# Encoder block on one core: turns and the norm's spread ahead of the first column sums, the first scale summed as columns, another order of loads, two ring slots filled early

## The chip, the cores and the metric

The kernel runs on one core of a Trainium2 chip. The metric is the device time of one execution in microseconds; for one core that is the time of this core. Its engines are TensorE (PE), VectorE (DVE), ScalarE (ACT), GpSimd (POOL) and SyncE (SP). SP and POOL issue the loads. Every engine works through its own instructions in order and waits on semaphores for the others.

## What is computed

One layer of a streaming-encoder block on x of 512 tokens by 1024, conditioned on a vector c:

```python
mod = (silu(c) @ ada_w + ada_b).reshape(b, 9, 1024)   # sh1, sc1, g1, sh2, sc2, g2, sh3, sc3, g3
h = rmsnorm(x, norm_ffn1_g) * (1 + sc1) + sh1
x = x + 0.5 * g1 * ((silu(h @ w1) * (h @ w3)) @ w2)   # 1024 -> 2816 -> 1024
h = rmsnorm(x, norm_mix_g) * (1 + sc2) + sh2
...                                                   # projection, short conv, 4-head attention, projection
h = rmsnorm(x, norm_ffn2_g) * (1 + sc3) + sh3
x = x + 0.5 * g3 * ((silu(h @ v1) * (h @ v3)) @ v2)
return rmsnorm(x, final_norm_g)
```

All is float32. The change touches the beginning alone: `silu(c) @ ada_w` for sc1 and sh1, the first norm, and the first tiles of `h @ w1` and `h @ w3`.

## The kernel before

The model dimension lies on the partitions, in eight tiles of 128 by 512 tokens. A product of full precision is made of three products on operands split into a high part (rounded, made by ACT) and a low part (the rest, made by DVE): `three`, L860. A unit is a weight tile of 128 by 1024 (`raw`, loaded by SP at L320; `wh`, its high part, L437 or L548; `wl`, its low part, L1400). Unit n alternates between two buffers, so the load of unit n waits for the low part of unit n-2. The up part of the first FFN takes two units per output tile: tile 0 is units 0 and 1, tile 1 is units 2 and 3, and so on.

The opening makes the modulation of the first FFN. `ada_start` holds sc1 and sh1's weights in four groups g: 0 and 1 are the halves of the scale sc1, 2 and 3 the halves of the shift sh1. Each group comes in four loads of 512 KB (L310), each with two of the eight k tiles. Of groups 0 and 1 the even k are PE's and the odd k are DVE's; of groups 2 and 3 all k are DVE's.

- DVE's share is `start_chunk` (L1623 for the first k, L1626 for the others): it adds `ada_start * silu_c` into `acc`. Each chunk waits for the one before it of its group.
- PE's share is `start_rows` (L1006): a product with one column of `silu_c` as the stationary operand and 512 moving columns, which gives one row of 512. ACT copies the row to `ada_rows` (`row_copy`, L543), and PE turns it into four columns with four products of one partition (L1018).
- `start_sum` (L1018 and L1023) adds the sums over `acc` as columns, and `start_mod` (L1634, L1642) on DVE makes `mods` and the norm's factors `a_cols` of it.

Tile 0 is computed from the norm without the shift (`plain_u`, L1651, makes it; `plain_steps`, L1032, are its float32 products on `raw_first`), and the shift's share is added later by `bias_step` (L1049). Tile 1 is `second_steps`: three products per k on `hh` (ACT, `shifted_hi`, L552) and `hl` (DVE, `shifted_lo`, L1657), which need the shift. Tiles 2 to 21 follow in a loop (`up_tile`).

PE also turns x (`turn_x`, L983): six of the eight tiles as the tokens land, the last two (`turn_last`) when ACT has copied the banks they need. It turns the small vectors (bias, gains) that POOL loads into `vec1` and `vec2` (L1059, L1061), and spreads the norm's factors over the partitions (`norm_spread`, L901).

POOL loads the other modulation weights into a ring of four slots (`ada_ring`, L402), 512 KB each, which DVE works through in the loop (L1466, L1468). The first four of these loads wait for `bias_done`, the last bias step, since the tile `raw_first` lies on slots 0 and 1 of the ring:

```python
(raw_first,), _ = place(region + 2 * FT * 4 * SEQ, ("raw_first", [P, 2, UW], F32))   # the ring's address
...
pool.wait_ge(bias_done, 1)
with pool.Fori(0, N_MOD - 2) as j:
    for k in range(DT):
```

The order of all this is written out by hand, engine by engine; there is no planner.

Of the kernel before, what the change touches and what calls it, by code (L numbers as in the profile page):

```python
# [26 lines left out]
P = 128  # L27
# [9 lines left out]
UW = 1024  # L37
# [60 lines left out]
def hybrid_block(nc, x, c, positions, ada_w, ada_b, norm_ffn1_g, ffn1_w1, ffn1_w3, ffn1_w2, norm_mix_g,  # L98
                 w_in, conv_w, q_norm_g, w_uq, kv_norm_g, w_ukv, out_norm_g, w_out, norm_ffn2_g,
                 ffn2_w1, ffn2_w3, ffn2_w2, final_norm_g, consts, out):  # L100
    with ExitStack() as ctx:
# [74 lines left out]
        (raw_first,), _ = place(region + 2 * FT * 4 * SEQ, ("raw_first", [P, 2, UW], F32))  # L176
# [122 lines left out]
        def _(sp):  # L299
# [5 lines left out]
            def start_load(g):  # L305
# [3 lines left out]
                for i in range(4):  # L309
                    sp.dma_start(ada_start[:, DT * v + 2 * i:DT * v + 2 * i + 2, half * HALF_COLS:(half + 1) * HALF_COLS],  # L310
                                 adav[:, 2 * i:2 * i + 2, col:col + HALF_COLS]).then_inc(start_landed[g][i], 16)
# [25 lines left out]
            start_load(1)  # L337
            sp.dma_start(raw_first[:, 1, :].rearrange("p (k f) -> p k f", k=DT), w3v[0][:, :, 0:P]).then_inc(first_landed[1], 16)
            start_load(2)
            start_load(3)  # L340
            load(U_A1 + 2, 0, w1v[0][:, :, P:2 * P])
            load(U_A1 + 3, 1, w3v[0][:, :, P:2 * P])
# [39 lines left out]
        def _(pool):  # L382
# [14 lines left out]
            pool.wait_ge(bias_done, 1)  # L397
            with pool.Fori(0, N_MOD - 2) as j:
                for k in range(DT):

                    pool.wait_ge(ada_step, ADA_START + j * DT + k - 3)
# [29 lines left out]
        def _(act):  # L431
# [106 lines left out]
            def row_copy(g):  # L538

                act.wait_ge(row_done, g + 1)  # L540
                if g > 0:
                    act.wait_ge(ada_direct, g)
                act.activation(ada_rows[0:1, :], pb[ROW_BANK[g]][0:1, :], ACT.Copy).then_inc(row_copied, 1)  # L543

# [9 lines left out]
            for k in range(DT - 2):  # L554
                copy_x(k)
            row_copy(0)
            copy_x(DT - 2)
            copy_x(DT - 1)
            row_copy(1)
# [294 lines left out]
        def _(pe):  # L854
# [146 lines left out]
            def start_rows(g, ks):  # L1001

                v, half = divmod(g, 2)
                for k in ks:
                    pe.wait_ge(start_landed[g][k // 2], 16)
                    ins = pe.matmul(pb[ROW_BANK[g]][0:1, :], silu_c[:, k:k + 1],  # L1006
                                    ada_start[:, DT * v + k, half * HALF_COLS:(half + 1) * HALF_COLS],
                                    start=k == ADA_ON_PE[g][0], stop=k == ADA_ON_PE[g][-1])
                    if k == ADA_ON_PE[g][-1]:
                        ins.then_inc(row_done, 1)  # L1010

            def start_sum(g):

                half = g % 2
                if g < 2:
                    pe.wait_ge(row_copied, g + 1)
                    for col in range(HALF):
                        pe.matmul(pb[ROW_BANK[g]][:, col:col + 1], ada_rows[0:1, col * P:(col + 1) * P], one_col[0:1, :],  # L1018
                                  start=col == 0, stop=False, skip_group_check=True)
# [26 lines left out]
            def bias_step(k):  # L1046

                for b in range(2):
# [3 lines left out]

            pe.wait_ge(siluc_ready, 1)
            start_rows(0, ADA_ON_PE[0])
            turn_last(DT - 2)
            turn_last(DT - 1)
# [5 lines left out]
                         ident[0:V_COLS - V_ROWS1, 0:V_COLS - V_ROWS1]).then_inc(vec_turned, 1)  # L1062
            pe.wait_ge(consts_landed, 16)
            start_sum(0)
            pe.wait_ge(vec_ready, 3)
            norm_spread(N_FFN1)
            pe.wait_ge(x_copied, 3)
            start_rows(1, ADA_ON_PE[1])
            pe.wait_ge(x_copied, 6)
            plain_steps(0, (0,))  # L1070
            start_sum(1)
            plain_steps(0, (1, 2, 3))
# [324 lines left out]
        def _(dve):  # L1397
# [263 lines left out]
            for k in ADA_ON_DVE[0]:  # L1661
                start_chunk(0, k)
# [3 lines left out]
            dve.wait_ge(vec_ready, 3)  # L1666
            start_chunk(1, 1)
            start_mod(0)
            start_chunk(1, 3)
            plain_u(0)  # L1670
            start_chunk(1, 5)
            plain_u(1)
            start_chunk(1, 7)
            plain_u(2)
            plain_u(3)
# [5 lines left out]
            for k in range(2, DT):  # L1681
# [406 lines left out]
```

## Time and profile before

| | |
|---|---|
| median of 3 runs | 1006.18 us (1004.42 to 1006.41) |
| the profiled execution | 1003.93 us |
| its span, first to last instruction | 1002.3 us |
| PE busy | 983.8 us |
| DVE busy | 549.4 us |
| ACT busy | 349.9 us |
| POOL busy | 51.9 us |
| bytes moved by DMA | 128.93 MB |

The span is that of the profiled execution; the rows below are all from it, in microseconds from its start. In a timeline a row is a run of like instructions of an engine: when it starts, how long it takes from the start of the first to the end of the last, the engine (SPq is SP's queue), the source line, the operation, the tiles, how many instructions, and in brackets how long the engine was idle before it and what ended that. A float32 product is recorded as two matmuls. Matmuls overlap at their ends, so the time of a step is best read from start to start.

### The profile page before, as it was taken

What the parts mean: (1) busy time and instruction counts of PE and PEld (TensorE: products, weight loads), DVE (VectorE), ACT (ScalarE), POOL (GpSimd) and SP (SyncE); (2) the same over time, 40 slices, a digit from 0 to 9 for tenths busy, and PEclk for the clock granted to TensorE, in tenths of its full rate; (3) what the DMA queues carried; (4) which work ended last, traced back from release to release, by engine and by line L of the source; (5) the groups of instructions that cost most, each with busy time, mean ns of one, the idle gap of its engine ahead of it and who ended that gap; (6) DMA issues with size and microseconds to landing.
All of it is one profiled execution on the core that took longest, in us unless ns stands there. A gap on an engine that the chain in (4) does not pass through costs nothing.

```text
span 1002.3 us, 13157 instructions
## 1 busy us (share of the span) xinstructions
PE 983.8 (98%) x4524; PEld 807.8 (81%) x4524; DVE 549.4 (55%) x772; ACT 349.9 (35%) x542; POOL 51.9 (5%) x79
## 2 busy tenths in 40 slices
PE   7999999999999999999999999999999999999997
PEld 4678888888888888888888887788888888888886
DVE  3867876787676445754475548754334344433332
ACT  5243323232342232531256534533323223323222
POOL 2011111011000000000000320000000000000000
PEclk9999999999999999999999999999999999999999
DMA  9757866686453333233221212232333323333232
GB/s 328 247 183 237 272 200 207 202 270 214 140 177 98 97 97 99 75 84 101 68 70 41 85 43 85 84 105 85 103 97 91 105 85 103 96 96 96 81 113 85
DMA packets 180493, 128.93 MB, mean 129 GB/s; under 512 B 5376, under 2 KB 168002, under 8 KB 180464
## 3 DMA queue, kind: packets, MB, share of 16 engines
q1 hardware_dynamic: 172064, 98.98, 33.1%
q0 software_dynamic: 8400, 29.58, 8.9%
q8 instruction: 17, 0.28, 0.1%
q14 instruction: 12, 0.10, 0.0%
HBM read 126.44 MB, written 2.10 MB: 128 GB/s over the span
## 4 chain that ended last, share of the span: by engine, by line
PE 89%; DVE 4%; SPq 2%; DMA 2%; ACT 1%; issue 1%; DVEq 0%; ACTq 0%
PE pb L860 86%; DMA raw<-in_ffn_w_dram 2%; SPq L310 2%; DVE wl L1400 1%; PE pb L901 1%; DVE hl L1432 1%; DVE ubuf L1439 1%; ACT wh L437 1%; PE pb L883 0%; PE pb L1380 0%; DVE ptl L1921 0%; PE pb L1191 0%; DVE acc L1626 0%; PE pb L939 0%; PE pb L933 0%
## 5 line engine op out<-in xcount | busy, mean ns | idle before, releaser
L860 PE MATMUL pb<-hh,wh 128*128 128x512 f32 x880 | 345.9, 393 | 4.4 <-DVE wl L1400 2.5
L860 PE MATMUL pb<-hh,wl 128*128 128x512 f32 x880 | 342.8, 389 | 0.0
L860 PE MATMUL pb<-hl,wh 128*128 128x512 f32 x880 | 342.5, 389 | 0.0
L1400 DVE TENSOR_TENSOR wl<-raw,wh 128x1024 fp32r<-128x1024 f32 x156 | 191.0, 1224 | 239.4 <-ACT wh L437 239.0
L437 ACT ACTIVATE wh<-raw 128x1024 fp32r<-128x1024 f32 x159 | 168.3, 1059 | 441.0 <-PE pb L860 432.9
L860 PEld LDWEIGHTS pb<-hh,wh 128*128 128x128 f32 x880 | 165.3, 188 | 42.0 <-issue 3.8
L860 PEld LDWEIGHTS pb<-hh,wl 128*128 128x128 f32 x880 | 165.2, 188 | 34.7
L860 PEld LDWEIGHTS pb<-hl,wh 128*128 128x128 f32 x880 | 165.3, 188 | 33.1
L860 PE MATMUL pb<-gh,wh 128*128 128x512 f32 x368 | 143.4, 390 | 0.0
L860 PE MATMUL pb<-gh,wl 128*128 128x512 f32 x368 | 143.2, 389 | 0.0
L860 PE MATMUL pb<-gl,wh 128*128 128x512 f32 x368 | 143.2, 389 | 0.0
L860 PEld LDWEIGHTS pb<-gh,wl 128*128 128x128 f32 x368 | 69.1, 188 | 14.3
L860 PEld LDWEIGHTS pb<-gh,wh 128*128 128x128 f32 x368 | 69.1, 188 | 14.3
L860 PEld LDWEIGHTS pb<-gl,wh 128*128 128x128 f32 x368 | 69.1, 188 | 14.2
L1468 DVE SCALAR_TENSOR_TENSOR acc<-ada_ring,silu_c,acc 128x1024 f32<-128x1024 f32 x49 | 62.8, 1281 | 1.2
L1503 DVE TENSOR_TENSOR gbuf<-sbuf,pb 128x512 f32<-128x512 f32 x40 | 27.4, 686 | 55.5 <-PE pb L860 55.5
L402 POOL DMA_DIRECT2D ada_ring<-in_ada_w_dram x56 | 29.6, 528 | 258.8 <-DVE acc L1466 123.8
L446 ACT ACTIVATE sq<-xres 128x512 f32 (+1 forms) x24 | 15.1, 632 | 78.1 <-DVE xres L1513 77.9
L1513 DVE SCALAR_TENSOR_TENSOR xres<-pb,half_gates,xres 128x512 f32<-128x512 f32 (+1 forms) x16 | 12.0, 749 | 37.7 <-PE pb L860 37.7
L486 ACT ACTIVATE gh<-gbuf 128x512 f32 x40 | 25.3, 633 | 13.0 <-DVE gbuf L1503 13.0
L1506 DVE TENSOR_TENSOR gl<-gbuf,gh 128x512 f32 (+1 forms) x40 | 27.3, 684 | 0.1
L1497 DVE TENSOR_TENSOR sbuf<-sigb,pb 128x512 f32<-128x512 f32 x40 | 27.2, 680 | 0.2
(259 smaller groups left out, 715.3 us busy)
## 6 DMA issues: line engine op xcount, KB each, us to landing
raw<-in_ffn_w_dram SPq DMA_DIRECT2D x102, 512.0 KB, 3.8
ada_ring<-in_ada_w_dram POOLq DMA_DIRECT2D x56, 512.0 KB, 5.1
raw<-in_ffn_w_dram SPq DMA_DIRECT2D x32, 448.0 KB, 3.4
raw<-in_w_in_dram SPq DMA_DIRECT2D x17, 512.0 KB, 3.9
ada_start<-in_ada_w_dram SPq DMA_DIRECT2D x16, 512.0 KB, 9.2
raw<-in_w_out_dram SPq DMA_DIRECT2D x8, 512.0 KB, 3.4
x_nat<-in_x_dram SPq DMA_DIRECT2D x4, 512.0 KB, 5.0
out_dram<-o_nat SPq DMA_DIRECT2D x4, 512.0 KB, 3.7
```

Of the source, the lines that this page charges most:

```text
L310: sp.dma_start(ada_start[:, DT * v + 2 * i:DT * v + 2 * i + 2, half * HALF_COLS:(half + 1) * HALF_COLS], adav[:, 2 * i:2 * i + 2, col:col ...
L402: pool.dma_start(ada_ring[:, k % 4, :], adav[:, k, bass.ds(j * D_MODEL + 2 * D_MODEL, D_MODEL)]) \
L437: act.activation(wh[par][:, :], raw[par][:, :], ACT.Copy).then_inc(hi_ready, 1)
L446: act.activation(sq[:, slot, :], src, ACT.Square).then_inc(sq_ready, 1)
L486: act.activation(gh[:, bass.ds(i, 1), :], gbuf[:, :].unsqueeze(1), ACT.Copy).then_inc(gh_ready, 1)
L860: last = pe.matmul(o, a, b, start=start and j == 0 and t == 0, stop=stop and j == len(pairs) - 1 and t == 2)
L1400: dve.tensor_tensor(wl[par][:, :], raw[par][:, :], wh[par][:, :].bitcast(F32), ALU.subtract).then_inc(lo_ready, 1)
L1468: dve.scalar_tensor_tensor(out=acc[:, :], in0=src, scalar=silu_c[:, k:k + 1], in1=acc[:, :], op0=ALU.mult, op1=ALU.add).then_inc(ada_step, 1)
L1497: dve.tensor_tensor(sbuf[:, :], sigb[:, :], pb[0][:, :], ALU.mult).then_inc(s_ready, 1)
L1503: dve.tensor_tensor(gbuf[:, :], sbuf[:, :], pb[1][:, :], ALU.mult).then_inc(g_ready, 1)
L1506: dve.tensor_tensor(gl[:, bass.ds(i, 1), :], gbuf[:, :].unsqueeze(1), gh[:, bass.ds(i, 1), :].bitcast(F32), ALU.subtract).then_inc(gl_read ...
L1513: dve.scalar_tensor_tensor(out=xd, in0=pb[bank][:, :].unsqueeze(1), scalar=gate, in1=xd, op0=ALU.mult, op1=ALU.add).then_inc(x_upd, 1)
```

## The change

It has five parts, all before the loop over tiles 2 to 21.

1. PE's order at the head: the two vector turns come first, then the first column step, the spread of the norm, and the last two turns of x between column steps. DVE copies the vectors before its chunks of group 0.
2. `start_rows` becomes `start_columns`: PE's even k of groups 0 and 1 are summed as columns at once, four products per k with a 128x128 block of `ada_start` as the stationary operand and one column of `silu_c` moving. The row copies of ACT and the products of L1018 go. In group 1 the column steps stand between plain steps.
3. SP's order of loads: the first load of group 2 goes ahead of the second half of `raw_first`, and unit 2's load goes ahead of the last two loads of group 3.
4. DVE's order: `plain_u` and chunks alternate; chunks of group 3 stand between the `shifted_lo` of the first half, ahead of the split of unit 3.
5. `raw_first` moves to the ring's slots 2 and 3, and POOL fills slots 0 and 1 once the shift is complete (`mods_ready`); slots 2 and 3 still wait for `bias_done`.

```diff
-        (raw_first,), _ = place(region + 2 * FT * 4 * SEQ, ("raw_first", [P, 2, UW], F32))
+        (raw_first,), _ = place(region + 2 * FT * 4 * SEQ + 2 * 4 * D_MODEL, ("raw_first", [P, 2, UW], F32))
...
             start_load(1)
+            start_load(2, (0,))
             sp.dma_start(raw_first[:, 1, :].rearrange("p (k f) -> p k f", k=DT), w3v[0][:, :, 0:P]).then_inc(first_landed[1], 16)
-            start_load(2)
-            start_load(3)
+            start_load(2, (1, 2, 3))
+            start_load(3, (0, 1))
             load(U_A1 + 2, 0, w1v[0][:, :, P:2 * P])
+            start_load(3, (2, 3))
             load(U_A1 + 3, 1, w3v[0][:, :, P:2 * P])
...
-            pool.wait_ge(bias_done, 1)
+            pool.wait_ge(mods_ready, 2)
             with pool.Fori(0, N_MOD - 2) as j:
                 for k in range(DT):
 
+                    if k == 2:
+                        pool.wait_ge(bias_done, 1)
...
-            for k in range(DT - 2):
+            for k in range(DT):
                 copy_x(k)
-            row_copy(0)
-            copy_x(DT - 2)
-            copy_x(DT - 1)
-            row_copy(1)
...
-            def start_rows(g, ks):
+            def start_columns(g, ks):
 
                 v, half = divmod(g, 2)
                 for k in ks:
                     pe.wait_ge(start_landed[g][k // 2], 16)
-                    ins = pe.matmul(pb[ROW_BANK[g]][0:1, :], silu_c[:, k:k + 1],
-                                    ada_start[:, DT * v + k, half * HALF_COLS:(half + 1) * HALF_COLS],
-                                    start=k == ADA_ON_PE[g][0], stop=k == ADA_ON_PE[g][-1])
-                    if k == ADA_ON_PE[g][-1]:
-                        ins.then_inc(row_done, 1)
+                    for col in range(HALF):
+                        at_ = half * HALF_COLS + col * P
+                        pe.matmul(pb[ROW_BANK[g]][:, col:col + 1], ada_start[:, DT * v + k, at_:at_ + P], silu_c[:, k:k + 1],
+                                  start=k == ADA_ON_PE[g][0] and col == 0, stop=False, skip_group_check=True)
...
-                if g < 2:
-                    pe.wait_ge(row_copied, g + 1)
-                    for col in range(HALF):
-                        pe.matmul(pb[ROW_BANK[g]][:, col:col + 1], ada_rows[0:1, col * P:(col + 1) * P], one_col[0:1, :],
-                                  start=col == 0, stop=False, skip_group_check=True)
...
-            pe.wait_ge(siluc_ready, 1)
-            start_rows(0, ADA_ON_PE[0])
-            turn_last(DT - 2)
-            turn_last(DT - 1)
...
+            pe.wait_ge(siluc_ready, 1)
+            start_columns(0, (0,))
+            pe.wait_ge(vec_ready, 3)
+            norm_spread(N_FFN1)
+            turn_last(DT - 2)
+            start_columns(0, (2,))
+            turn_last(DT - 1)
+            start_columns(0, (4, 6))
             pe.wait_ge(consts_landed, 16)
             start_sum(0)
-            pe.wait_ge(vec_ready, 3)
-            norm_spread(N_FFN1)
-            pe.wait_ge(x_copied, 3)
-            start_rows(1, ADA_ON_PE[1])
             pe.wait_ge(x_copied, 6)
             plain_steps(0, (0,))
+            start_columns(1, (0,))
+            plain_steps(0, (1,))
+            start_columns(1, (2,))
+            plain_steps(0, (2,))
+            start_columns(1, (4,))
+            start_columns(1, (6,))
             start_sum(1)
-            plain_steps(0, (1, 2, 3))
+            plain_steps(0, (3,))
...
-            for k in ADA_ON_DVE[0]:
-                start_chunk(0, k)
             dve.wait_ge(vec_turned, 2)
...
             dve.wait_ge(vec_ready, 3)
+            for k in ADA_ON_DVE[0]:
+                start_chunk(0, k)
+            start_mod(0)
+            plain_u(0)
+            plain_u(1)
             start_chunk(1, 1)
-            start_mod(0)
             start_chunk(1, 3)
-            plain_u(0)
+            plain_u(2)
             start_chunk(1, 5)
-            plain_u(1)
+            plain_u(3)
             start_chunk(1, 7)
-            plain_u(2)
-            plain_u(3)
             start_chunk(2, 0)
             start_chunk(2, 1)
             start_mod(1)
             for k in range(HALF, DT):
                 plain_u(k)
-            for k in range(2, DT):
-                start_chunk(2, k)
-            for k in range(3):
-                start_chunk(3, k)
+                start_chunk(2, k - 2)
+            start_chunk(2, 6)
+            start_chunk(2, 7)
+            start_chunk(3, 0)
+            start_chunk(3, 1)
             start_mod(2)
+            start_chunk(3, 2)
+            shifted_lo(0)
             start_chunk(3, 3)
-            shifted_lo(0)
             split_lo(U_A1 + 2, 0)
             for k in range(1, HALF):
                 shifted_lo(k)
+                start_chunk(3, 3 + k)
             split_lo(U_A1 + 3, 1)
-            for k in range(HALF, DT):
-                start_chunk(3, k)
+            start_chunk(3, DT - 1)
             start_mod(3)
```

## Rows read from the trace of the kernel before

**Rows 1.** The page: busy times, and granted clock in 40 slices (9: 90% or more).

```profile
PE 983.8 (98%) x4524; PEld 807.8 (81%) x4524; DVE 549.4 (55%) x772; ACT 349.9 (35%) x542; POOL 51.9 (5%) x79
...
PEclk9999999999999999999999999999999999999999
```

**Rows 2.** By stretch: length, busy PE, PEld, DVE, ACT, POOL, clock, DMA share, GB/s.

```profile
30.00:35.00 5.00, 5.00 (x13) 2.21 (x12) 4.48 (x8) 0.00 (x0) 0.00 (x0) 1.00 1.06 376
...
69.10:150.00 80.90, 80.74 (x357) 66.78 (x358) 64.57 (x73) 24.68 (x38) 12.14 (x23) 1.00 0.76 236
```

**Rows 3.** The chain that ended last, 24 to 48 us: start, length, what.

```profile
24.77 13.50 DMA raw<-in_ffn_w_dram
...
38.30 1.07 ACT wh L548
...
39.39 1.23 DVE wl L1400
...
47.02 1.07 PE pb L1023 x8
```

**Rows 4.** Timeline of PE, 16 to 41 us.

```profile
16.23 1.10 PE L983 MATMUL pb<-kst,x_nat 128*128 128x128 f32 x8
...
17.43 1.03 PE L1018 MATMUL pb<-kst,ada_rows 1*128 1x1 f32 x8
18.39 1.05 PE L1023 MATMUL pb<-kst,acc 128*128 128x1 f32 x8
19.30 1.14 PE L901 MATMUL pb<-kst,rrms 128*128 128x128 f32 x8
20.37 3.59 PE L1006 MATMUL pb<-ada_start,silu_c 128*1 128x512 f32 x8
...
36.36 0.95 PE L1023 MATMUL pb<-kst,acc 128*128 128x1 f32 x8
37.17 3.68 PE L1032 MATMUL pb<-ada_start,raw_first 128*128 128x512 f32 x8
40.72 0.47 PE L860 MATMUL pb<-hh,wh 128*128 128x512 f32 x1
```

**Rows 5.** Timeline of PE, 41 to 51 us: the second step, and the fifth.

```profile
41.85 0.48 PE L860 MATMUL pb<-hh,wh 128*128 128x512 f32 x1
...
50.03 0.47 PE L860 MATMUL pb<-hh,wh 128*128 128x512 f32 x1 [0.46 <-DVE hl L1657]
```

**Rows 6.** Timelines of DVE and of ACT (the last row), 19 to 43 us.

```profile
19.48 0.16 DVE L1634 TENSOR_TENSOR mods<-pb,vcol 128x4 f32<-128x4 f32 x1 [0.55 <-PE pb L1023]
...
20.54 0.74 DVE L1651 SCALAR_TENSOR_TENSOR ada_start<-xres,a_cols,pb 128x512 f32<-128x512 f32 x1
21.19 0.75 DVE L1626 SCALAR_TENSOR_TENSOR acc<-ada_start,silu_c,acc 128x512 f32<-128x512 f32 x1
...
30.05 5.01 DVE L1626 SCALAR_TENSOR_TENSOR acc<-ada_start,silu_c,acc 128x512 f32<-128x512 f32 x6
...
40.53 2.07 DVE L1657 SCALAR_TENSOR_TENSOR hl<-ada_start,mods,hh 128x512 fp32r<-128x512 f32 x3
...
37.55 0.72 ACT L552 ACTIVATE hh<-ada_start,mods 128x512 fp32r<-128x512 f32 x1 [12.96 <-DVE mods L1634]
```

**Rows 7.** POOL's last vector load in the timeline, and its time to landing.

```profile
5.62 0.51 POOL L393 DMA_DIRECT2D vec<-in_conv_w_dram  x1
...
vec<-in_conv_w_dram POOLq DMA_DIRECT2D x1, 6.0 KB, 5.4
```

**Rows 8.** Chain from unit 6's load; landing of the last early ring load; a lone load.

```profile
57.40 8.64 DMA raw<-in_ffn_w_dram
...
69.11 10.95 PE pb L860 x47
...
ada_ring<-in_ada_w_dram POOLq DMA_DIRECT2D x1, 512.0 KB, 7.0
...
raw<-in_ffn_w_dram SPq DMA_DIRECT2D x1, 512.0 KB, 3.8
```

More of the change, by code:

```diff
@@ L303, in _, with start_load @@
                 sp.dma_start(x_nat[:, t, :], x[0][t * P:(t + 1) * P, :]).then_inc(x_landed[t], 16)
-            def start_load(g):
+            def start_load(g, pieces=range(4)):
                 v, half = divmod(g, 2)
                 col = (D_MODEL if v == 0 else 0) + half * HALF_COLS
-                for i in range(4):
+                for i in pieces:
                     sp.dma_start(ada_start[:, DT * v + 2 * i:DT * v + 2 * i + 2, half * HALF_COLS:(half + 1) * HALF_COLS],
@@ L536, in copy_x @@
                 act.activation(xres[:, k, :], pb[X_BANK[k]][:, :], ACT.Copy).then_inc(x_copied, 1)
[L538 to L543, printed above, removed]
             def second_split(n):
```

## The prediction

> **What bounds the kernel now.** I read the clock and the busy shares first [rows 1]: TensorE (PE) is busy for 98% of the span at full granted clock in all 40 slices. So a change to the opening pays only through PE's own queue: by work taken off it, or by waits between its instructions. Then the busy time by stretch [rows 2]: from 69.1 to 150 us PE has 0.16 us without work, so what is gained before 69 us is carried to the end unless a new wait eats it. Then the chain of waits [rows 3]. Up to 38.3 us it consists of loads that follow each other: the first second-tile weight load (tile `raw`, unit 2) is issued at 24.77 and lands at 38.28. It is cut into its high part on ACT at 38.30 and its low part on DVE at 39.39, and PE's first three-product step follows at 40.72 [rows 4]. Yet PE has by then just finished its own queue: four plain steps begin at 37.17 and take 8 records of 0.43 (3.68 less an end of 0.25), so PE is free at 40.6. Loads and PE queue end together: to gain, a change has to shorten both, and this one touches both.
>
> **The terms on PE's queue.** (a) Row form against column form. A row step of the first scale is one 1x512 product, two records of 0.43, 0.86 us (the 8 records from 20.37 take 3.59, less an end, [rows 4]). A column step is four products of 128x128 with one moving column, 8 records. The nearest row is the group of 8 that sums `acc` the same way: it starts at 18.39 and the next group at 19.30, 0.91 us; another starts at 36.36 with the next at 37.17, 0.81 us; the dearest relative is the spread, 1.07 us from 19.30 to 20.37 [rows 4], whose moving 128 columns the new steps don't have. I take 0.89, near the first: 8 steps cost 8 x 0.03 = 0.24 more than now, with bounds of -0.4 and +1.7. (b) Gone: two groups of 8 that turn the row into columns (L1018), 17.43 to 18.39 [rows 4], 0.96 each, 1.9 us, and the two ACT copies and their handshakes. Net off PE's queue: 1.7 us.
>
> **The opening, worked forward.** PE has turned the first 24 tiles of `x` at 10.9. Now it takes the four row steps as their loads land (3.4 us of work, and the rest up to 16.23 is waiting), then the last turns and the vector turns (16.23 to 17.43), L1018, and the sum at 18.39 to 19.30 [rows 4]. After the change the work between 10.9 and the end of that sum is: vector turns and last turns 1.2, spread 1.07, 4 column steps 3.6, sum 0.91, together 6.8, so it ends near 17.7. No load stands in the way, since each column step comes at or after the time at which its row step found its load. The new gate at the head is the small vectors: the last is issued by POOL at 5.62 and takes 5.4, 11.0 us [rows 7]; cost 0.1. The first scale is thus ready 1.6 us earlier: DVE reads it at 17.9 and not 19.48 [rows 6].
> Two DVE operations of 0.2, the first `plain_u` of 0.74 and a handshake follow, so PE's first plain step can start at 19.1. PE **pauses 1.4 us** there (17.7 to 19.1), as the row steps of the second half, which filled it, now stand behind. From 19.1: 4 column steps 3.6, sum 0.9, 16 plain steps at 0.86 13.8, third sum 0.9, together 19.2: PE is free at 38.3, against 40.6 now, 2.3 us earlier.
> **First three-product step.** The third sum ends at 34.9. DVE reads it (35.3), ACT writes the first `hh` (0.72, [rows 6]) and the high part (1.07, [rows 3]), which ends at 37.2. Its load landed at 38.28; two loads of 512 KB that stood before it now stand behind it, 1.05 MB at 376 GB/s [rows 2] or 2.8 us, so it lands near 35.5, half a microsecond before ACT asks for it. On DVE stand chunk, `lo0`, chunk (3 x 0.66 and 0.27 of waiting for `hh`) and the low part 1.23 [rows 3]: 38.8, so PE starts at 38.9, after a wait of 0.6 (it now waits 0.1 to 0.4 there). Against 40.72: **1.8 us earlier**.
> **Second half of the weights.** Four steps with the bias products take 1.13 each (40.72 to 41.85, [rows 4, 5]): PE is at 43.4. DVE now puts a chunk behind each `lo`: 6 x 0.66 = 4.0 and the low part 1.23, 44.0. A wait of 0.6 is **new** here. In its favour: six chunks in a row take 5.01, 0.85 each as each waits for the one before, while `lo` operations in a row take 0.66 (three in 2.07, the last 0.75) and an operation of an alternating pair about the same (20.54 to 21.19) [rows 6]; so the last chunk is done at 44.9 and the fourth sum, which starts at 47.02 now [rows 3], starts at 45.4 with no wait for DVE: two steps of 3 x 0.23 after 44.0. From there to the step at 50.03 [rows 5] the same operations follow in both: **1.65 us earlier**. The third chunk-wait that goes (0.3 before 47.02) is already in this. My forward working of the unchanged order by the same prices ends 0.1 us late at 57.5; the changed one ends 1.75 us before it. I take 1.75.
> **Ring slots.** The load for unit 6 is issued at 57.40 behind four 512 KB ring loads and takes 8.64; a lone one takes 3.8 [rows 8]. It lands at 66.05, and through ACT, DVE's split and `sbuf` PE starts at 69.11, where it would have gone on at 68.5: 0.6 us. With two slots filled at 46 to 51 us (no weight load is due then), two ring loads stand before it. By the rows, 8.64 less two of about 1.2 (the difference of 8.64 and 3.8 over four) is 6.2. The wait vanishes below 8.0, so I count **0.6 us**. The moved `raw_first` costs nothing; POOL's wait inside the loop is met from the second turn on. Behind the waiting POOL instruction stand only further ring loads.
> The Trainium skill (DMA: Bandwidth & Descriptors, Queues, rings and completion order) says that each DMA engine takes packets in turn from the queues that have work. By that the load at 57.40 would share with POOL's queue half and half and land some 3 us after issue; the wait at 68.5 would then not be the ring's doing, and this term would be 0. The row speaks against it: 8.64, and the last ring load took 7.0 [rows 8].
>
> **The rivals.**
> *A, as reckoned*: 1.75 + 0.6 = 2.35 us off; the rows allow 1.6 to 2.8. Chance 0.50.
> *B, one term only*: the ring term stays out (1.75 off), or column steps cost 1.07 like the spread, which takes 1.45 from the first term (0.9 off). For it: the second new wait leaves DVE, and not PE, in charge from 38.9 to 44. Gain 0.3 to 1.6 us, chance 0.24.
> *C, more*: column steps at 0.81 give 0.45 more, and if the loads run ahead by one slot the waits at 38.9 and 44.0 shrink by up to 1.2. Gain 2.8 to 4.2 us. Chance 0.15.
> *D, slower by column loads*: if a weight load can't lie under the product before it, each record shows its full length. The last record of the group at 18.39 lasts 0.25 (1.05 less 7 starts of 0.114), against 0.114 from start to start [rows 4]. Place: all 8 column steps. Price: each 0.1 us per step costs 0.8; it decides from 1.18 us per step on (0.89 + 2.35/8). At 0.25 per record a step is 2.0 us, 8.9 us dearer in all, and the kernel 6.5 us slower. Against it: 8 records within 0.91 us in the same form [rows 4]. Chance 0.04.
> The Trainium skill (TensorE: Matmul & The Clock Gate, Part 3) says that a weight load overlaps a running product only where the row groups differ, which these don't; that is D. The rows bear out the overlap instead.
> *E, the head waits or nothing changes*: the vector turn now stands first in PE's queue. A last vector after 11.0 us moves all by as much; at 13.4 us the gain is gone, later it is a loss. Or the shift is lost in the loads: from 30 us on, each load is a fixed point, and if the swapped weight load lands at 38 as now, the first three-product step stays at 40.7, and the sum is 0 to 0.6 off. Chance 0.07.
>
> **How the numbers follow.** The span is 1002.3, the profiled execution took 1003.93 and the median is 1006.18, 2.25 above it. 2.35 off: 1001.6 for a profiled execution, 1003.8 for the median. The case's own range is 1003.2 to 1004.8. For 8 in 10 I leave out the far end of C and most of D and E, and allow for the spread of the runs shown (2 us): 1002.2 to 1006.2. Above or below 0.2% is 2.0 us, about what a measurement of this kernel can tell from no change. A lies above that in 0.38 of its 0.50, C wholly: faster 0.53. B, the rest of A and 0.05 of E: 0.41. D and 0.02 of E: 0.06.
>
> **What would show it.** Right: the first DVE `mods` near 17.9; a PE pause of about 1.4 us ahead of its first plain step; three-product steps from 38.9, with a wait near 44; the step that stood at 50.03 near 48.3; no wait at the third tile (69.11 becomes 66.8 or so); ring loads of two slots at 46 to 47 us. Wrong: groups of 8 column records above 1 us, a vector turn after 11.3, a weight load that lands after 36.5, or the wait for `sbuf` still there. A granted clock below full in the new pause would break the whole sum; PE waits for loads in the first slices too, and they are at full clock [rows 1].

## The result and the profile after

The changed kernel takes 1010.78 us (median of 9, 1010.32 to 1015.41) against 1005.96 us for the kernel before (median of 9, 1004.23 to 1006.42). The ratio is 1.0061, 95% interval [1.0053, 1.0069]: 0.6% slower, where 0.2% faster was forecast. Its profiled execution took 1010.88 us with a span of 1009.2. In the experiments below, one of the four executions of x2 took 1662.23 us at a mean granted clock of 0.555; nothing here explains it, and it is left out of x2's numbers.

The clock comes first, as [rows 1] did. From the page of the changed kernel, busy time and granted clock in 40 slices:

```profile
PE 989.5 (98%) x4556; PEld 818.5 (81%) x4556; DVE 548.5 (54%) x772; ACT 348.1 (34%) x540; POOL 51.9 (5%) x79
...
PEclk8799999999999999999999999999999999999999
```

The first two slices are not at full clock. The same by stretches of 5 us (start:end, length, busy time of PE, its weight loads, DVE, ACT and POOL with their instructions, granted clock, DMA share, GB/s):

```profile
10.00:15.00 5.00, 4.35 (x38) 4.12 (x38) 2.34 (x6) 4.87 (x10) 0.00 (x0) 1.00 1.05 378
15.00:20.00 5.00, 4.04 (x29) 3.95 (x28) 1.68 (x5) 0.60 (x1) 0.00 (x0) 0.70 1.10 355
20.00:25.00 5.00, 4.64 (x12) 3.12 (x13) 4.90 (x9) 0.00 (x0) 0.00 (x0) 0.50 1.09 362
25.00:30.00 5.00, 5.00 (x17) 3.45 (x16) 0.92 (x2) 0.00 (x0) 0.00 (x0) 0.50 1.06 378
30.00:35.00 5.00, 5.00 (x21) 4.49 (x22) 0.75 (x3) 0.00 (x0) 0.00 (x0) 0.50 1.09 352
35.00:40.00 5.00, 5.00 (x10) 2.15 (x9) 4.95 (x8) 0.00 (x0) 0.00 (x0) 0.75 1.01 315
```

A mean of 0.70 over 5 us is 3 us at half clock (1.2 GHz in place of 2.4), 0.75 is 2.5 us. So the clock was low from 17.0 to 37.5 us, 20.5 us long. In the profiled execution of the kernel before all of these stretches are at 1.00. The timeline of PE shows what it did before the fall and what each step cost at either level (start, length, line, operation, tiles, count):

```profile
11.80 1.02 PE L1001 MATMUL pb<-silu_c,ada_start 128*128 128x1 f32 x8 [0.65 <-DMA ada_start<-in_ada_w_dram]
12.69 1.14 PE L894 MATMUL pb<-kst,rrms 128*128 128x128 f32 x8
13.66 0.60 PE L976 MATMUL pb<-kst,x_nat 128*128 128x128 f32 x4
14.10 0.95 PE L1001 MATMUL pb<-silu_c,ada_start 128*128 128x1 f32 x8
14.91 0.63 PE L976 MATMUL pb<-kst,x_nat 128*128 128x128 f32 x4
15.38 1.95 PE L1001 MATMUL pb<-silu_c,ada_start 128*128 128x1 f32 x16
17.19 1.85 PE L1010 MATMUL pb<-kst,acc 128*128 128x1 f32 x8
20.36 2.05 PE L1019 MATMUL pb<-ada_start,raw_first 128*128 128x512 f32 x2 [1.32 <-DVE ada_start L1644]
22.20 1.71 PE L1001 MATMUL pb<-silu_c,ada_start 128*128 128x1 f32 x8
23.77 2.05 PE L1019 MATMUL pb<-ada_start,raw_first 128*128 128x512 f32 x2
...
43.53 0.95 PE L1010 MATMUL pb<-kst,acc 128*128 128x1 f32 x8
44.34 3.68 PE L1019 MATMUL pb<-ada_start,raw_first 128*128 128x512 f32 x8
48.11 0.47 PE L853 MATMUL pb<-hh,wh 128*128 128x512 f32 x1
...
53.17 0.51 PE L853 MATMUL pb<-hh,wh 128*128 128x512 f32 x1 [0.35 <-DVE wl L1393]
...
57.59 0.47 PE L853 MATMUL pb<-hh,wh 128*128 128x512 f32 x1 [0.46 <-DVE hl L1650]
```

From 11.8 us PE is never without an instruction until 19.0, and the clock falls at 17.0. Between these times there is no product of 512 columns: PE runs column steps of one moving column, the spread, and turns. The first sum, whose row in [rows 4] is 1.05 long, is 1.85 long here. The step that stood at 50.03 [rows 5] stands at 57.59, 7.56 us later. The span is 6.9 us longer, less than that since the wait for `sbuf` at 69.11 [rows 8] is gone. From 69 us on the two kernels have the same time without work (0.12 against 0.16 up to 150 us).

### The profile page after: what moved, and what is told of

It reads as the page before. It is cut to its first block, busy times and chain, and to the rows that moved or that the text cites. A ratio compares the mean times of both kernels' runs of the same rounds, so it can differ in the third digit from the quotient of the medians.

```text
span 1009.2 us, 13219 instructions
## 1 busy us (share of the span) xinstructions
PE 989.5 (98%) x4556; PEld 818.5 (81%) x4556; DVE 548.5 (54%) x772; ACT 348.1 (34%) x540; POOL 51.9 (5%) x79
## 4 chain that ended last, share of the span: by engine, by line
PE 93%; DVE 3%; ACT 1%; issue 1%; DMA 1%; SPq 0%; ACTq 0%; DVEq 0%
PE pb L853 87%; PE pb L1019 2%; PE pb L1001 1%; DVE wl L1393 1%; PE pb L894 1%; DMA ada_start<-in_ada_w_dram 1%; DVE hl L1425 1%; DVE ubuf L1432 1%; PE pb L1010 0%; PE pb L876 0%; PE pb L1373 0%; DVE ptl L1916 0%; PE pb L1184 0%; ACT wh L441 0%; DVE acc L1619 0%
```

## The experiments

On the measure: the kernel before itself has two groups of times, and each execution comes with its mean granted clock. Of 29 executions of it that ran beside x12 to x14, the 10 with a mean clock of 0.999 or 1.0 have a median of 1004.5 us, the 19 with 0.997 or 0.998 one of 1006.2. The profiled execution [rows 1] was of the first group.

### Which part makes the clock fall

The head is what PE does from 10.7 us to its first plain step. A stretch is called light below when PE runs only one-column products, turns and the spread in it, and no product of 512 columns. Theory L: the column form makes the head too light for the clock. Theory O: the new order at the head does. First the column form alone, put into the kernel before:

```diff
-            start_rows(0, ADA_ON_PE[0])
+            start_columns(0, ADA_ON_PE[0])
...
-            start_rows(1, ADA_ON_PE[1])
+            start_columns(1, ADA_ON_PE[1])
```

> The kernel before with the column form in place of the row form, and nothing else: same order of steps, loads, DVE work and ring. Theory L: the granted clock falls to half near 17 us or earlier, since column steps of 0.9 us with waits for loads between them are lighter still than in the changed kernel; 6 to 9 us slower than before, ratio 1.006 to 1.009. Theory O: full clock throughout, and 1.7 us less work on the queue: ratio 0.998.

1012.92 us, ratio 1.008 [1.006, 1.010]. Busy time and clock by stretch:

```profile
10.00:15.00 5.00, 3.84 (x26) 3.47 (x24) 2.05 (x4) 3.81 (x9) 0.00 (x0) 0.87 1.05 375
15.00:20.00 5.00, 5.00 (x24) 4.66 (x24) 0.95 (x3) 1.20 (x2) 0.00 (x0) 0.50 1.09 357
...
35.00:40.00 5.00, 5.00 (x10) 2.10 (x9) 4.58 (x8) 0.00 (x0) 0.00 (x0) 0.74 1.03 268
```

A mean of 0.87 is 1.3 us at half clock: it falls at 13.7 us and stays low to 37.6. The waits for loads between the column steps (0.41, 0.45 and 0.30 us) are like those between the row steps of the kernel before (0.42, 0.36 and 0.36), so they aren't what differs. The form alone is enough, in an order that held full clock with rows. Next, rows in both groups in the changed kernel:

```diff
-            start_columns(0, (0,))
+            start_rows(0, (0,))
...
             def start_sum(g):
...
+                if g in (0, 1):
+                    pe.wait_ge(row_copied, g + 1)
+                    for col in range(HALF):
+                        pe.matmul(pb[ROW_BANK[g]][:, col:col + 1], ada_rows[0:1, col * P:(col + 1) * P], one_col[0:1, :],
+                                  start=col == 0, stop=False, skip_group_check=True)
```

> The changed kernel with the row form back in both groups of the scale (with ACT's copies and the two groups that turn the row); all else as changed, the order at the head too. Theory L (the one-column products of the head are too light a load for TensorE, and the granted clock falls to half at 17 us for 20 us): full clock in every stretch, and the time is that of the kernel before less 2.35 us plus 1.7 us for what returns to the queue: about 1005.3 against 1005.96, ratio 0.999. Theory O (it is the order at the head: turns, spread and vector turns bunched from 10.7 us on, and the pause ahead of the first plain step): the clock still falls to half before 20 us, ratio 1.005 or more.

1009.08 us, ratio 1.0041 [1.0027, 1.0055]. The early fall is gone, but a short one remains (by stretch):

```profile
15.00:20.00 5.00, 4.23 (x22) 2.20 (x22) 0.89 (x2) 1.19 (x3) 0.00 (x0) 1.00 1.10 358
20.00:25.00 5.00, 3.67 (x9) 0.78 (x8) 4.30 (x9) 0.00 (x0) 0.00 (x0) 0.71 1.09 358
25.00:30.00 5.00, 5.00 (x11) 1.01 (x10) 2.37 (x4) 0.00 (x0) 0.00 (x0) 0.95 1.05 379
```

Neither theory alone: 3.4 us at half clock (2.9 and 0.5) in place of 20.5, and it begins behind the pause, not at 17. So the form sets the long fall, and the new order with its waits costs a short one of its own. The profiled execution is one of the two best of five: their mean clocks go from 0.998 down to 0.994, and 0.994 is by an estimate 10 to 12 us at half clock (0.6% of 1008 us is 6 us of lost clock, less up to 1 that an execution without a fall shows too). And the clock is not all of the 1.0041. In this order PE also waits for ACT's copy of each row, 0.68 us for the second and 0.77 for the first (timeline of PE):

```profile
18.49 1.02 PE L1030 MATMUL pb<-kst,ada_rows 1*128 1x1 f32 x8 [0.77 <-ACT ada_rows L547]
```

The two waits cost 1.45 us where the fall costs 1.7. x3 below has the first of them too. The two mixed forms complete the table.

```diff
-            start_columns(0, (0,))
+            start_rows(0, (0,))           # x3: group 0 only
...
-            start_columns(1, (0,))
+            start_rows(1, (0,))           # x11: group 1 only
```

> The changed kernel with the row form back in the first group alone; the second group stays in column form, where its steps alternate with plain steps of 512 columns. Theory L: what matters is the light stretch from 10.7 to 17 us; with rows in it the clock stays full, and with plain steps between them the later column steps do no harm: 1.5 us faster than before, ratio 0.9985. If any column step below a certain density does harm, the clock falls later, between 20 and 30 us, ratio above 1.003. Theory O: the clock falls near 17 us, ratio 1.005.

> The changed kernel with the row form back in the second group alone; the first group, the one of the head, stays in column form. With x1 and x3 it completes the table of both forms in both groups. Theory L: the head up to 17 us is as light as in the changed kernel, so the clock falls there, near 17 us; but from 20 us on all steps have 512 columns, so it comes back sooner than after 20 us: 5 to 6 us less time at half clock than the changed kernel, ratio 1.003 to 1.004 against its 1.006. If the length at half clock is fixed, ratio 1.007.

| groups 0, 1 | ratio | at half clock in the profiled execution |
|---|---|---|
| columns, columns (changed) | 1.0061 [1.0053, 1.0069] | 17.0 to 37.5 |
| rows, columns (x3) | 1.0077 [1.0060, 1.0094] | 21.4 to 38.5 |
| columns, rows (x11) | 1.0030 [1.0017, 1.0044] | 16.8 to 23.7, and 30.5 to 37.3 |
| rows, rows (x1) | 1.0041 [1.0027, 1.0055] | 3.4 us between 22.1 and 25.5 |

In these four profiled executions the first group's form goes with when the clock falls: with columns near 17, with rows behind the pause. The second group's form goes with how long it stays: with columns 17 us or more, with rows 3.4 or 6.9 (in x11 twice). x11 came out as forecast. x3's forecast of 0.9985 missed: the clock fell behind the pause as in x1, and stayed low under the column steps between the plain steps. Its row for 30 to 35 us, by stretch, shows that PE is busy all the time, mostly with weight loads (4.89 of 5), at half clock:

```profile
30.00:35.00 5.00, 5.00 (x25) 4.89 (x23) 0.00 (x0) 0.00 (x0) 0.00 (x0) 0.50 1.10 353
```

### More work, less time

If light products are the cause, adding idle full ones must help. A filler is one float32 product of 512 columns, 0.86 us, whose result nobody reads:

```diff
+            filler(6, 0)
             start_columns(0, (0,))
...
-            start_columns(0, (4, 6))
+            filler()
+            start_columns(0, (4,))
+            filler()
+            start_columns(0, (6,))
+            filler()
...
             start_sum(0)
+            filler()
```

> The changed kernel with five idle products of 512 columns (identity on x, float32, 0.86 us each, results unused) put between the column steps of the head: one ahead of the first column step, one ahead of and one behind the third, one behind the fourth, one in the pause ahead of the first plain step. It computes the same and TensorE has 4.3 us more work, some 1.7 us of which lies in waits. Theory L (too few columns stream through the array in the head): the clock stays full and the kernel gets faster by its added work, about -2.35 + 2.6 us against before, ratio 1.000. If it falls at a later light stretch (the last two column steps of the second group and the sum behind them), ratio 1.002 to 1.005. If the cause isn't the lightness of the head, the clock falls as in the changed kernel and the added work is paid in full: ratio 1.009.

1006.79 us, ratio 1.0016 [1.0006, 1.0026]: 4.3 us of added work, and 4 us faster than the changed kernel. The profiled execution (1004.49 us) is at full clock in every stretch of the opening, of which three:

```profile
15.00:20.00 5.00, 5.00 (x31) 3.73 (x31) 0.75 (x1) 0.91 (x2) 0.00 (x0) 1.00 1.10 358
20.00:25.00 5.00, 4.64 (x23) 2.84 (x22) 3.68 (x8) 0.00 (x0) 0.00 (x0) 1.00 1.10 358
25.00:30.00 5.00, 5.00 (x37) 4.16 (x36) 3.31 (x7) 0.00 (x0) 0.00 (x0) 1.00 1.05 379
```

Of the ten executions two had a mean clock of 0.999 (1004.5 and 1004.6), the others 0.996 to 0.998 (1005.6 to 1009.2). So five fillers shorten the time at half clock in all ten and prevent a fall in two. Those two also test the rest of the forecast: with the fillers it was 0.25 us more than the kernel before, and 1004.5 and 1004.6 stand beside a median of 1004.5 of the 13 executions of the kernel before at 0.999 or 1.0 in that set. A single filler, in the pause:

```diff
             start_sum(0)
+            filler()
```

> The changed kernel with one idle product of 512 columns in the pause of 1.3 us ahead of the first plain step, and nothing else. Theory L: the clock has already fallen at 17 us, 2 us before the pause, so filling it does not keep the clock: still half from 17 us on, ratio 1.005 to 1.007. If the pause was the cause (and the record of the clock only early), full clock and ratio 0.998.

1009.29 us, ratio 1.0031 [1.0010, 1.0052]. The profiled execution is as forecast, half clock from 17 us on (0.74, then 0.50). But its nine executions spread from 1003.75 to 1014.27: three had a mean clock of 0.996 (1003.75, 1004.06 and 1007.03), the others 0.985 to 0.991. A mean of 0.996 is by the same estimate 6 to 8 us at half clock, so with this one filler the time at half clock can be much shorter. That was not expected, and the ratio is below the forecast 1.005 to 1.007. Where these shorter falls lay no trace shows. And rows with both waits filled, against x1:

```diff
             start_rows(0, (4, 6))
+            filler()
...
             start_sum(0)
+            filler()
```

> Rows in both groups in the changed order (which fell to half clock for 3.4 us at about 21 us) with two of the idle products in its two waits: one while ACT copies the first row, one ahead of the first plain step. Theory L: its waits of 0.8 and 1.3 us with only groups of one-column products between them are what is too light; filled, the clock stays full throughout, and the time is 0.3 to 0.7 us below the kernel before, ratio 0.9995. Otherwise the fall to half stays, ratio 1.004.

1008.04 us, ratio 1.0027 [1.0017, 1.0036]. The fall behind the pause is gone, and another of 3.4 us came right behind the next light stretch, where the second row is copied, turned and summed (29.7 to 32.3 us in its timeline), so the forecast 0.9995 missed:

```profile
25.00:30.00 5.00, 4.71 (x10) 0.71 (x9) 3.36 (x6) 0.25 (x1) 0.00 (x0) 1.00 1.06 380
30.00:35.00 5.00, 4.61 (x20) 3.05 (x21) 2.47 (x6) 0.34 (x1) 0.00 (x0) 0.75 1.09 352
35.00:40.00 5.00, 5.00 (x12) 2.16 (x11) 4.79 (x8) 0.00 (x0) 0.00 (x0) 0.91 0.96 299
```

### The parts that leave PE's work at the head alone

The ring alone, in the kernel before:

```diff
-        (raw_first,), _ = place(region + 2 * FT * 4 * SEQ, ("raw_first", [P, 2, UW], F32))
+        (raw_first,), _ = place(region + 2 * FT * 4 * SEQ + 2 * 4 * D_MODEL, ("raw_first", [P, 2, UW], F32))
...
-            pool.wait_ge(bias_done, 1)
+            pool.wait_ge(mods_ready, 2)
...
+                    if k == 2:
+                        pool.wait_ge(bias_done, 1)
```

> The kernel before with the move of raw_first and the two early ring loads alone. By the prediction's term: the wait of 0.6 us ahead of the third tile goes and nothing else changes, ratio 0.9994. If the load for unit 6 was held up by something other than the ring loads, the wait stays and the ratio is 1.0000.

1004.52 us against 1005.38, ratio 0.9991 [0.9981, 1.0001]. The load that took 8.64 in [rows 8] takes 5.4, and PE's waits no longer have one for `sbuf`. The first row is from its DMA issues (KB, us to landing), the second its only PE wait between 50 and 80 us (us in total, times, longest):

```profile
raw<-in_ffn_w_dram SPq DMA_DIRECT2D x1, 512.0 KB, 5.4
...
PE pb L862 <- DVE hl L1659: 0.4, 1, 0.4
```

The four executions at 0.999 or 1.0 took 1003.35 to 1004.17 (median 1003.4), against a median of 1004.6 of the kernel before beside them, and the profiled spans are 1001.7 and 1002.3. So the mechanism is there and its size is 0.6 to 1.2 us; the interval of the ratio just touches 1. The same with the order of loads and of DVE, and rows on PE in the order of before:

> TensorE and ACT as in the kernel before (rows, its order), and from the change the order of loads, the ring slots and DVE's order from the first scale on. Full clock is expected by every theory. By the prediction's terms: 0.6 for the ring, and 0.3 to 0.4 for the fourth sum, which no longer waits for a row of chunks; nothing before 40.7 us, where TensorE's own queue sets the time. Ratio 0.9990. If the alternating order of DVE costs something (the second low part comes later), ratio 0.9995 to 1.0005.

1004.90 us, ratio 0.9993 [0.9984, 1.0002]. Its fourth sum has no chunk to wait for, but a wait of 0.37 for the second low part stands two steps ahead of it, as worked out (timeline of PE):

```profile
47.50 0.51 PE L864 MATMUL pb<-hh,wh 128*128 128x512 f32 x1 [0.37 <-DVE wl L1404]
49.01 0.95 PE L1027 MATMUL pb<-kst,acc 128*128 128x1 f32 x8
```

It is not told apart from x4, nor from no change. Full clock was expected by every theory, and that missed: only 3 of its 11 executions are at 0.999 or more, and the profiled one (0.998) has 3.4 us at half clock:

```profile
15.00:20.00 5.00, 4.86 (x32) 3.84 (x33) 1.43 (x5) 1.67 (x3) 0.00 (x0) 0.93 1.09 361
20.00:25.00 5.00, 5.00 (x13) 1.44 (x12) 3.73 (x6) 0.00 (x0) 0.00 (x0) 0.73 1.10 354
```

PE's order is that of the kernel before, and the clock is low from 19.3 to 22.7 us, beginning inside this order's light stretch (the spread runs at 19.3). No execution of the kernel before with a mean of 0.998 was profiled; this is the nearest trace of what its slower group does.

### Trying to cover the light stretch with real work

The kernel before has a light stretch of its own from 16.2 to 20.4 us [rows 4], and x7 has the same one. x9 moved two row steps of x7 into it. x10 put the second group's row steps into the waits of the changed order, and two of DVE's chunks ahead of the first scale:

```diff
-            start_sum(0)
+            start_sum(0, lambda: start_rows(1, (0,)))     # x9: behind L1018, ahead of the sum
+            start_rows(1, (2,))
...
             norm_spread(N_FFN1)
```

```diff
+            start_rows(1, (0,))                           # x10
...
             start_sum(0)
+            start_rows(1, (2,))
...
+            start_rows(1, (4,))
             plain_steps(0, (0,))
...
```

> x7_orders_rows with two of the second group's row steps (0.86 us each, 512 columns, real work that was due 2 us later) moved into the light stretch of the head from 17 to 21 us: one between the products that turn the first row and the sum, one between the sum and the spread. No work is added, and the first plain_u has 2 us of slack. Theory L: the executions of the kernel before, and of x7, with a mean granted clock of 0.997 to 0.998 are ones in which the clock fell for 3.4 us in just this stretch, at a cost of 1.7 us; they get rare or vanish, and the median falls to 1003.5 to 1004.3, ratio 0.998. If that fall has nothing to do with the light stretch, the share of executions at 0.998 stays above a half and the ratio is that of x7, 0.9993.

> The changed order at the head with rows in both groups (x1), and the second group's row steps moved into its two waits: one ahead of the products that turn the first row, two ahead of the first plain step, two of DVE's chunks ahead of the first scale. It has neither the pause of 1.3 us nor a stretch of one-column products of more than 1 us. Theory L: full clock in most executions, and by the prediction's terms 0.6 (ring), 0.3 (fourth sum) and 0.4 (waits for loads filled by turns and spread) below the kernel before at full clock: median 1003.3 to 1004.2, ratio 0.998. If the order at the head (vector turns, turns and spread between row steps) is itself what lowers the clock, it still falls at 21 us, ratio 1.003.

x9: 1009.33 us, ratio 1.0031 [1.0021, 1.0040], no execution above a clock of 0.998. The forecast failed. Part of it is a wait that the edit opened and that I had not seen (timeline of PE):

```profile
30.55 1.05 PE L1029 MATMUL pb<-kst,acc 128*128 128x1 f32 x8 [1.55 <-DVE acc L1633]
```

The second sum waits 1.55 us for DVE's chunks, which came later with the later first scale, and a second fall follows it. The first fall, between 20 and 25 us, isn't explained by that. x10: 1005.22 us, ratio 1.0002 [0.9992, 1.0011] against a forecast of 0.998; 7 of 12 executions at 0.998 or more (1004.15 to 1005.27), 5 at 0.995 or 0.996 (1007.4 to 1007.9). The profiled one is of the five, with 6.8 us at half clock between 20 and 30 us. Better than x1 in the same order, and no better than the kernel before.

x9 raised the question whether a row step is a weak cover since it has only one stationary column. Two products of equal length in the same two places of the kernel before, full or thin:

```diff
-            start_sum(0)
+            start_sum(0, lambda: filler(ident))              # x12; x13: filler(silu_c[:, 0:1])
+            filler(ident)                                    # x13: filler(silu_c[:, 0:1])
```

> The kernel before with two idle products put into its light stretch from 17 to 21 us (between the products that turn the first row and the first sum, and between that sum and the spread). Each has a stationary block of 128x128 and 512 moving columns, 0.86 us. Same sums as before, 1.7 us more work on TensorE's queue. Theory F (what keeps the clock is products with many stationary and many moving columns; a row step, with one stationary column, is nearly as light as a one-column product): the falls of the kernel before go in nearly all executions, so its two groups of times (1004.4 and 1006.1) become one near 1006.1, all at a mean clock of 0.999 or 1.0; ratio 1.0005 to 1.001. Theory L as first put (only moving columns count): the same. If the clock falls nevertheless: 1007.5 and more.

> The same two places, the same 512 moving columns and the same 0.86 us each, but with one stationary column, the form of a row step. Theory F: this doesn't hold the clock: it falls in most executions as in x9, in some twice, and the time is 1007.5 to 1009.5, ratio 1.002 to 1.004. Theory L (moving columns alone count): no difference from x12, ratio 1.0005 to 1.001.

x12: 1006.82 us, ratio 1.0017 [1.0007, 1.0026]. x13: 1006.55 us, ratio 1.0013 [1.0003, 1.0024]. The ratios don't differ. At a mean clock of 0.999 or more are 9 of 11 executions of x13 and 5 of 11 of x12, against 10 of 29 of the kernel before. So theory F falls: the thin form, which by it would lose the clock in most executions, held it in 9 of 11. For the full form both theories had expected nearly all executions at full clock, and that missed: 5 of 11 isn't told apart from 10 of 29. Both pay for 1.7 us of added work. In x12's profiled execution the fall has moved behind the second light stretch, to 29.2 us (0.92 over 25 to 30 us). Last, three fillers of 192 columns in the waits for loads of x4's head:

```diff
-            start_rows(0, ADA_ON_PE[0])
+            start_rows(0, (0,))
+            for k in (2, 4, 6):
+                filler(ident, 7, 0, 192)
+                start_rows(0, (k,))
```

> The ring change alone (x4) with three full idle products of 192 columns (0.33 us each) in the three waits for loads between the row steps of the head, 0.36 to 0.42 us long in the kernel before. They should lie inside these waits and cost nothing. Theory F: more full products ahead of the light stretch make the fall of 3.4 us rarer: x4 had it in half of its executions (1003.4 without, 1005.2 with); share below a quarter, median near 1003.5, ratio 0.998. If only the light stretch itself counts, the share and the median of x4 stay: ratio 0.9991.

1004.90 us, ratio 0.9990 [0.9982, 0.9999]; 5 of 12 executions at 0.999 or 1.0 (1003.4 to 1003.8), and of the other seven one took 1004.2 and six 1005.6 to 1005.9. The profiled one has 3.4 us at half clock between 20 and 25 us. The share of executions below 0.999 is about that of x4 (7 of 12, 6 of 10): no help is seen from work ahead of the light stretch. x4 and x14 have the two lowest ratios of the study, 0.1% below the kernel before.

## Why the prediction was wrong

**The step that failed** is the one that had no line in the sum: "at full granted clock in all 40 slices". I read the clock of the kernel before and took it for a property of the kernel. It depended on what the change takes out: with one-column products in place of 512-column ones the clock was at half for 20.5 us. The price of a column step at full clock was right, and a fall of the clock had no price. The last sentence of the prediction names a clock below full as what would break the sum, but puts it into the pause, gives it no chance, and looks at waits alone; the clock fell 2 us ahead of the pause, under a queue without a wait. No rival described it, so the range had no room for it.

**The loss, recomputed.** At half clock PE does half: 20.5 us cost 10.25. Of the pause of 1.32 us half is no loss (0.66), as PE had nothing to do. 9.6 is left, against a miss of 9.3 us at the step of 57.59 (forecast 48.3, measured 57.59). The forecast for the whole, 2.35 us off, missed by 9.3 too (span 6.9 longer). So what remains beside the clock is within 0.3 us of the sum. That is a balance, not an experiment; x2 and x5 show the cause, and x5's two executions at 0.999 bear out the rest of the sum.

**The terms.** A column step: forecast 0.89; 0.89 (11.80 to 12.69) and 0.81 (14.10 to 14.91) at full clock, 1.57 at half (22.20 to 23.77). The first scale at 17.9: DVE read it at 19.08, of which 0.8 is the half clock (1.85 long where 1.05 is full clock) and 0.4 the first load, for which the first column step waited 0.65 to 11.8. The pause 1.4: 1.32. The first three-product step, 4.0 behind the end of the third sum: 3.77 (44.34 to 48.11); its load, which was to land near 35.5, had landed by 36.0. The new wait of 0.6 ahead of the second weights: 0.35, at 53.17. The wait ahead of the fifth step: 0.46, as before. The wait for `sbuf`: gone, in the changed kernel and in x4; the load took 5.3 and 5.4 where 6.2 was worked out.

The prediction also weighs that the two load queues take turns, and reads this as half and half, by which the ring term would be 0. That reading doesn't hold: some 3 us to landing is less than even the lone load's 3.8. The load took 8.64 behind four ring loads, 5.4 behind two and 3.8 alone, so the ring loads do hold it up. Turns taken packet by packet aren't ruled out by that, for the packets are unequal. From the profile of x4 (queue, packets, MB), q1 being SP's and q0 POOL's:

```profile
q1 hardware_dynamic: 172064, 98.98, 33.1%
q0 software_dynamic: 8400, 29.58, 9.0%
```

A packet of POOL's carries 3.5 KB and one of SP's 0.58 KB on the average, so by an estimate from these two rows equal turns would give POOL's loads about six times as many bytes.

**The rivals.** D had weight loads that can't lie under the running product. The Trainium skill (TensorE: Matmul & The Clock Gate, Part 3) says so for equal row groups; with 8 records in 0.81 to 0.89 us, each load 0.19 long, the trace disagrees here as it did before. The sign of D came true, and nearly its size (6.5 us slower, where the span grew by 6.9), by another mechanism; that is chance. In C the column steps at 0.81 give 8 x 0.08 = 0.64 and not 0.45, which changes nothing here.

The Trainium skill (TensorE: Matmul & The Clock Gate, Why this matters for your kernels) advises against idle gaps between bursts of products, lest the clock falls. The changed kernel obeys it and its clock falls nevertheless: the row of 15 to 20 us has PE busy for 4.04 of 5, and the only wait in it comes after the fall. An instruction on PE at every moment from 11.8 us on didn't keep the clock here.

**The conversion to a median.** I added 2.25 us to go from the profiled execution to the median, as a neutral offset. Most of it, 1.7 us, goes with the clock: 19 of 29 executions of the kernel before have a mean of 0.997 or 0.998 and a median of 1006.2, where those at 0.999 or 1.0, like the profiled one, have 1004.5. [rows 1] is of one execution and can't show that; the mean clock of each execution does. The changed kernel has no such difference (1010.88 profiled, median 1010.78). So the forecast missed by 9.3 us for the profiled execution and by 7.0 for the median, and the 2.25 us made the miss look smaller.

**What stays open.** The first fall of x9: two steps of 512 columns lie in its stretch, and x13 with nearly the same sequence mostly held. No trace shows whether the slower executions of the kernel before have the fall that x7's trace has. And it is open why the clock of the same kernel falls in some executions and not in others. No run here tells whether that is how the loads land or something else.

## What to carry to other kernels

Before a change that turns wide products into one-column ones of the same length, or bunches turns and other narrow products, look for the stretches that are left without a 512-column product, and give a fall of the clock there a price (half of its length) and a chance. Here every profiled fall began in such a stretch or right behind one, if only of 1 us (the first of x9). Read the granted clock of several executions, not of the profiled one alone; two groups of times 0.2% apart can be a fall of some microseconds. A kernel that is 98% busy can lose more by light work than it gains by less work, and idle wide products in waits are a cheap way to test it.

## What the runs showed of the hardware

- The clock went from 2.4 to 1.2 GHz at 17.0 us under a queue that had been without a wait since 11.8, while PE ran one-column products, turns and the spread (changed kernel).
- Steps of 512 columns alternating with column steps didn't bring the clock back in the profiled execution of x3: it stayed low from 21.4 to 38.5 us with PE busy throughout, and returned only under plain steps alone.
- The stationary width made no difference to the time: 1 or 128 columns under the same 512 moving ones gave 1.0013 and 1.0017.
- In the profiled executions with one light stretch filled, the fall stood behind the next one: from 32.5 us in x6, from 29.2 in x12.
- A load of 512 KB by SP took 8.64 us behind four of POOL's, 5.4 behind two and 3.8 alone.
